# The first projection chunk of a transformer kernel, split in two by k and run between the modulation blocks

## What is computed

```python
mod = silu(c) @ w_ada + b_ada                    # 1024 -> 6144, in 12 blocks of 512 columns
shift1, scale1, gate1, shift2, scale2, gate2 = split(mod, 6)
h = rms_norm(x, norm1_g) * (1 + scale1) + shift1
proj = h @ w_in                                  # 1024 -> 5120, in 10 chunks of 512 columns
q_sb, k_sb, v_sb, q_mb, k_mb, v_mb, g_sb, g_mb = split(proj, ...)
...                                              # two attentions, gates, w_out, 64-expert mixture
...                                              # second block: mixer, memory attention, 16-expert mixture
```

## Time and profile before

| | |
|---|---|
| median of 3 runs | 1556.61 us (1556.6 to 1557.11) |
| the profiled execution, its own time | 1556.61 us |
| its span | 1554.8 us |
| PE busy | 1323.6 us (85%) |
| DVE busy | 545.9 us (35%) |
| ACT busy | 407.1 us (26%) |
| mean granted clock of TensorE | 0.929 |
| DMA | 337 GB/s on the mean over the span |

### The profile page before, as it was taken

One profiled execution on the slowest core, in us unless ns is written; L12 is line 12 of the kernel. 1 busy time (PEld: TensorE's weight loads), 2 busy tenths in 40 slices (PEclk: granted clock), 3 DMA queues, 4 the chain that ended last, 5 costly groups with the idle time before them and its releaser, 6 DMA issues.

```text
span 1554.8 us, 24390 instructions
## 1 busy us (share of the span) xinstructions
PE 1323.6 (85%) x10184; PEld 900.3 (58%) x10184; DVE 545.9 (35%) x1197; ACT 407.1 (26%) x624; POOL 0.2 (0%) x4
## 2 busy tenths in 40 slices
PE   6999998999999999999699999999666657557556
PEld 2888896656666665555488999999323113113112
DVE  3546665343333232321474775753301001001001
ACT  3457743111111111111264346453201000000001
POOL 0000000000000000000000000000000000000000
PEclk8999999899999999999999999999889678788878
DMA  9884759699999999999933544447999999999996
GB/s 364 275 290 172 279 198 403 274 393 385 422 421 415 420 416 420 416 418 421 389 139 114 212 163 163 164 165 292 409 422 417 422 421 418 422 422 419 422 422 250
DMA packets 119321, 523.53 MB, mean 337 GB/s; under 512 B 11032, under 2 KB 15544, under 8 KB 72120
## 3 DMA queue, kind: packets, MB, share of 16 engines
q1 hardware_dynamic: 115952, 519.17, 84.0%
q10 hardware_dynamic: 3272, 2.96, 0.6%
HBM read 520.85 MB, written 1.24 MB: 336 GB/s over the span
## 4 chain that ended last, share of the span: by engine, by line
PE 61%; DMA 17%; SPq 15%; DVE 3%; ACT 2%; issue 2%; DVEq 0%; ACTq 0%
PE psum L1975 17%; PE psum L2425 10%; SPq L663 7%; PE psum L2493 5%; SPq L670 5%; DMA ring<-in_w_up_e_dram 4%; DMA arena<-in_w_exp_down_dram 4%; PE psum L2361 4%; DMA ring<-in_w_exp_up_dram 4%; PE psum L2350 2%; DMA ring<-in_w_exp_down_dram 2%; SPq L674 2%; PE psum L2885 2%; PE psum L2222 1%; PE psum L1983 1%
## 5 line engine op out<-in xcount | busy, mean ns | idle before, releaser
L1975 PE MATMUL psum<-arena_r,ring_r 128*128 128x256 f32 x2400 | 289.0, 281 | 6.0 <-DVE arena_r L1145 3.1
L1975 PEld LDWEIGHTS psum<-arena_r,ring_r 128*128 128x128 f32 x2400 | 283.1, 188 | 12.2 <-issue 7.5
L2425 PE MATMUL psum<-ring,arena 128*32 128x256 f32 (+1 forms) x2304 | 183.9, 390 | 11.2 <-DMA ring<-in_w_up_e_dram 10.4
L1138 DVE TENSOR_TENSOR ring_r<-ring,ring_r 128x1024 fp32r<-128x1024 f32 x140 | 163.2, 1221 | 69.6 <-ACT ring_r L759 68.8
L2425 PEld LDWEIGHTS psum<-ring,arena 128*32 128x32 f32 (+1 forms) x2304 | 111.0, 123 | 76.2 <-issue 20.2
L2885 PE MATMUL psum<-ring,arena 128*32 128x512 f32 x720 | 109.5, 738 | 51.6 <-DMA ring<-in_w_exp_up_dram 46.3
L759 ACT ACTIVATE ring_r<-ring 128x1024 fp32r<-128x1024 f32 x140 | 137.5, 1050 | 27.8 <-DMA ring<-in_w_in_dram 13.4
L2902 PE MATMUL psum<-ring,arena 128*32 128x512 f32 x384 | 76.8, 834 | 66.1 <-DMA ring<-in_w_exp_down_dram 47.6
L2493 PE MATMUL psum<-ring,arena 128*32 128x512 f32 (+1 forms) x544 | 91.0, 617 | 3.4 <-DMA ring<-in_w_down_e_dram 2.5
L2885 PEld LDWEIGHTS psum<-ring,arena 128*32 128x32 f32 x720 | 22.2, 123 | 114.7 <-DMA ring<-in_w_exp_up_dram 64.5
L2902 PEld LDWEIGHTS psum<-ring,arena 128*32 128x32 f32 x384 | 18.7, 142 | 119.3 <-issue 89.8
(11 more groups left out here) (410 smaller groups left out, 1457.0 us busy)
## 6 DMA issues: line engine op xcount, KB each, us to landing
ring<-in_w_gate_e_dram SPq DMA_DIRECT2D x64, 1024.0 KB, 15.1
ring<-in_w_up_e_dram SPq DMA_DIRECT2D x64, 1024.0 KB, 14.3
ring<-in_w_down_e_dram SPq DMA_DIRECT2D x60, 1024.0 KB, 14.4
ring<-in_w_exp_gate_dram SPq DMA_DIRECT2D x45, 1024.0 KB, 26.2
ring<-in_w_exp_up_dram SPq DMA_DIRECT2D x45, 1024.0 KB, 26.0
ring<-in_w_exp_down_dram SPq DMA_DIRECT2D x40, 1024.0 KB, 26.6
ring<-in_w_in_dram SPq DMA_DIRECT2D x19, 2048.0 KB, 8.9
ring<-in_w_ada_dram SPq DMA_DIRECT2D x12, 2048.0 KB, 13.5
```

The lines of the kernel that those rows point to most:

```text
L1138: V.tensor_tensor(lo, whole, hi.bitcast(F32), ALU.subtract).then_inc(w_low, 1)
L1975: ins = product(lambda a_, b_, k, first, last: mm(ps[:, t * T:(t + 1) * T], a_[:, k, c], b_[:, k, :], start=first, stop=last), w, x, None ...
L2425: ins = mm(psum[c, 5, 256 * g:256 * g + 256], xg1[:, k, P * j + width * b:P * j + width * (b + 1)], weight(g, e, k), start=(k == 0), stop= ...
```

## The change

The four modulation blocks and the first projection chunk are loaded and multiplied in another order.

- SP issues ada0, ada1, the first half of in0 (k-tiles 0 to 3), ada2, ada3, the second half of in0. The blocks ada2 and ada3 go to two places in the arena that are free then (`ada_away`: buffers 11 and 12, and 4 and 5), not to the ring. So the ring's list is two slots shorter from there on, and in1 lands in slots that were never used. The load of the memory tokens, which go to buffer 11, waits for ada2's product.
- PE does ada0 and ada1 with their columns, then four matmuls 128x256 whose result is thrown away (`idle_products`), then the k-tiles 0 to 3 of in0 in three portions (24, 12 and 12 matmuls) with ada2 and ada3 between them, then k-tiles 4 to 7 (48).
- ACT copies ada2 and ada3 out behind the high parts of the first half, not ahead of them.

The core of the diff:

```diff
-CHUNKS_A = [("w_ada", 512 * ADA_ORDER[_j], 512, 8) for _j in range(ADA_FIRST)]
+ADA_RING = 2
+CHUNKS_A = [("w_ada", 512 * ADA_ORDER[_j], 512, 8) for _j in range(ADA_RING)]
...
+        ada_away = [buf(11, SLOT), buf(4, SLOT)]
...
+            for n in range(ADA_RING):
+                load(ring[:, SLOT_A[n], :], CHUNKS_A[n], load_a[SLOT_A[n]])
+            first_input_half(0, first_in)
+            for n in range(2):
+                load(ada_away[n], ("w_ada", 512 * ADA_ORDER[ADA_RING + n], 512, 8), load_away[n])
+            first_input_half(1, load_a[SLOT_A[IN_A[0]]])
             for n, spec in enumerate(CHUNKS_A):
+                if n <= IN_A[0]:
+                    continue
...
                 if n == IN_A[3]:
+                    full(sp, "ada2")
                     sp.dma_start(memN, a["mem_columns"].rearrange("p (k t) -> p k t", t=T)).then_inc(mem_in, 16)
...
             rms_act(1, rstd_of(1))
-            for n in range(3):
+            for n in range(2):
                 ada_copy(n)
             act.wait_ge(normed, 1)
             x_high_part("h1", 0)
-            ada_copy(3)
             high(0, (0, 1))
+            for n in (2, 3):
+                ada_copy(n)
             act.wait_ge(normed, 2)
...
+            def idle_products(ps, n):
+
+                for _ in range(n):
+                    mm(ps[:, 0:T], ones, cst[:, 0:T], start=True, stop=True)
...
-            for n in range(ADA_FIRST):
-                if n:
-                    if n == 3:
-                        pe.wait_ge(mod_ready, 1)
-                    columns(n - 1).then_inc(mod_full, 1)
...
+            for n in range(ADA_RING):
                 modulation(n, n)
-            columns(ADA_FIRST - 1).then_inc(mod_full, 1)
...
+                columns(n).then_inc(mod_full, 1)
+            idle_products(start("in0_0"), 4)
+            first_products(0, 0)
+            modulation(2, None)
+            first_products(0, 1, range(1))
+            pe.wait_ge(mod_ready, 1)
+            columns(2).then_inc(mod_full, 1)
+            modulation(3, None)
+            columns(3).then_inc(mod_full, 1)
+            first_products(0, 1, range(1, 2))
+            for j in range(2):
+                first_products(1, j)
```

More of the change, by code:

```diff
@@ L184 @@
 JOBS = ["rel"]
-JOBS += ["ms1", "sum1"] + [f"ada{_j}" for _j in range(ADA_FIRST)]
+JOBS += ["ms1", "sum1", "ada0", "ada1", "in0_0", "ada2", "in0_1", "ada3"]
 for _c in range(6):
-    JOBS += [f"in{_c}_{_j}" for _j in range(2)] + {3: ["ms0"], 4: ["sum0"]}.get(_c, []) + [f"ada{_j}" for _j in ADA_BEHIND.get(_c, ())]
+    JOBS += [f"in{_c}_{_j}" for _j in range(2) if _c] + {3: ["ms0"], 4: ["sum0"]}.get(_c, []) + [f"ada{_j}" for _j in ADA_BEHIND.get(_c, ())]
 for _p in range(PAIRS):
@@ L412, in build @@
         first_in = sem("first_input_half_loaded")
+        load_away = [sem(f"modulation_block_loaded{i}") for i in range(2)]
         load_ahead = sem("block_ahead_loaded")
@@ L537, in load @@
                     sp.dma_start(dst, a["w_gate_sh"][0].rearrange("(k p) f -> p k f", p=P)).then_inc(done, 16)
[L538 to L542, removed]
                 else:
@@ L558, in _, with first_input_half @@
             sp.dma_start(xT, a["x_columns"].rearrange("p (k t) -> p k t", t=T)).then_inc(x_in, 16)
+            def first_input_half(h, landed):
+                dst = ring[:, SLOT_A[IN_A[0]], :].rearrange("p (k c) -> p k c", k=KT)
+                sp.dma_start(dst[:, 4 * h:4 * h + 4, :], a["w_in"][0, 512 * h:512 * h + 512, 0:512].rearrange("(k p) c -> p k c", p=P))\
+                  .then_inc(landed, 16)
+            for n in range(ADA_RING):
[4 more added lines that the diff above has]
+            first_input_half(1, load_a[SLOT_A[IN_A[0]]])
             for n, spec in enumerate(CHUNKS_A):
+                if n <= IN_A[0]:
+                    continue
                 if SLOT_A[n] >= RING:
@@ L2059, in modulation @@
             def modulation(n, place, gives=None):
-                w = chunk_a(place, 512)
+                if ADA_RING <= n < ADA_FIRST:
+                    pe.wait_ge(load_away[n - ADA_RING], 16)
+                    w = ada_away[n - ADA_RING].rearrange("p (k c) -> p k c", k=KT)
+                else:
+                    w = chunk_a(place, 512)
                 if n == 0:
@@ L2075, in modulation @@
                     columns(n - 1, gives=(used_a, 1)).then_inc(mod_full, 1)
-                elif n != ADA - 2:
+                elif n != ADA - 2 and not ADA_RING <= n < ADA_FIRST:
                     full(pe, f"ada{n}")
@@ L2093, in _ @@
             norm_total(1, part_x)
-            for n in range(ADA_FIRST):
-                if n:
-                    if n == 3:
-                        pe.wait_ge(mod_ready, 1)
-                    columns(n - 1).then_inc(mod_full, 1)
-                modulation(n, n)
-            columns(ADA_FIRST - 1).then_inc(mod_full, 1)
[L2102 to L2121, removed]
@@ new lines, in _, with first_products @@
+            n0 = IN_A[9] - 8
+            def first_products(half, j, ts=range(2)):
+                hi, lo = PARTS["h1"]
+                w = chunk("a", IN_A[0], whole=False)
+                name = f"in0_{j}"
+                ps = bank(name) if half or j == 0 or ts[0] else start(name)
+                for t in ts:
+                    cols = slice((2 * j + t) * P, (2 * j + t + 1) * P)
+                    for k in range(4 * half, 4 * half + 4):
+                        if j == 0 and t == 0 and k % 2 == 0:
+                            pe.wait_ge(x_low, 4 * PART_AT["h1"] + k // 2 + 1)
+                            pe.wait_ge(w_low, k // 2 + 1)
+                        for i, (a_, b_) in enumerate(((w[0], hi), (w[0], lo), (w[1], hi))):
+                            ins = mm(ps[:, t * T:(t + 1) * T], a_[:, k, cols], b_[:, k, :], start=(t == 0 and k == 0 and i == 0),
+                                     stop=(k == KT - 1 and i == 2), skip_group_check=True)
+                if half:
+                    done(ins, name)
@@ L2125, in _ @@
                 w = chunk("a", IN_A[c], whole=False)
-                if c == 0:
-                    project_by_halves(w)
                 for j in range(2):
```

## The result

The change is slower, by 0.2 to 0.3%. In the first set of runs its median was 1562.81 us (1559.34 to 1563.65, 6 runs) against 1556.64 us before (1556.44 to 1557.11, 6 runs), a ratio of 1.0033, 95% interval 1.0021 to 1.0045. So the first set puts the change at +6.2 us and the second at +3.0, and the forecast of +4.0 (1560.6) lies between them; the first median alone lies 0.4 us above the range. They come from one trace of each kernel, though, and traces of one kernel differ too.

The account below looks back on a forecast made before the run. The prediction took the modulation weights' loads, then PE from 35.77 us on, to bound the kernel. in0's end moves from 49.63 to 53.6, +4.0 us, all passed on: 1556.61 + 4.0 = 1560.6 us, range 1556.8 to 1562.4.

Parts of the forecast that it names:

- one sign of being wrong that the prediction names: Behind in0: the prediction is wrong if later stages don't keep the shift; no size of its own.
- The path: In in0: the second half of h waits for ada3's later columns, PE idles 3.8 us, in0 ends 4.0 us later.
- the forecast of 53.6 us for in0's end: End of in0: last 48 products from 45.5 us, 24 slow and 24 fast, end at 53.6 against 49.63 before.
- The chain of DVE, ACT and DVE, 5.2 us: Ahead of each half of in0: from the columns' end to PE's first product takes 5.2 us.
- The first 24 products start at 28.1: Start of in0: DVE's step at 22.8 plus 5.3 gives 28.1 us, 7.7 us ahead of 35.77.
- 2.7 slow and 12 fast: 4.1 us: First 24 products of in0: 12 at the slow clock in 2.7 us, 12 fast in 1.4, ending at 32.2.
- The last 48 products, 8.1 us: Second half of in0: slow clock after PE's idling, 24 products slow in 5.3 us and 24 fast in 2.8.
- The price: ada3 is now behind them on PE. This is the term that decides.: PE before in0's second half: ada3's columns end at 40.3, 5.0 us later, 2.7 by the load alone.
- I pass on all of it: Behind in0's end: later stages, expert loads included, start later by the whole shift, so +4.0 us reaches the end.
- my rival: From about 311 us: expert loads set the end, their start isn't moved, shift vanishes: 1556.6, up to 1558; chance 0.09.
- The edits put at nothing: in1's split, the shorter ring and the memory tokens' wait: each nothing; in1's split, if late, under 1 us.

Follow-up runs that it names:

- e8: The change with the clock raised early, 10 idle products ahead of its first 24 products and 7 ahead of the last 48: 1556.55 us, ratio 1.0001.
- e11: The kernel before with the clock raised early as in e7, but three idle products instead of one just ahead of in0: 1554.96 us, ratio 0.9990.
- e5: The change once more, unaltered, in a second set of runs beside the kernel before: 1560.17 us median of 12, ratio 1.0021.
- e12: e1 (the change's loads, old order of PE and ACT) with idle products in PE's gaps: 1554.95 us, ratio 0.9993.
- e1: The change's loads and places only, with PE and ACT in the old order and no idle products: 1559.7 us, ratio 1.0018.
- e10: e11 with 23 idle products instead of three ahead of in0, a pure delay: 1560.54 us median of 7, 5.6 us above e11.
- e9: The kernel before once more, unaltered, one run with its trace: 1557.29 us.
- e4: The kernel before with idle products between the modulation blocks, 3 behind each of the first three blocks' columns: 1555.55 us, ratio 0.9992.
- e7: The kernel before with the clock raised early by idle products from 10 us on, in the waits for copies and behind columns: 1553.81 us, ratio 0.9980.
- e2: The change without its four idle products: 1560.93 us, ratio 1.0028.
- e3: The change with 11 idle products instead of 4 ahead of the first 24 products, and 8 more ahead of the last 48: 1560.52 us, ratio 1.0017.
- e6: The change with the 12 products between ada2's and ada3's products moved behind ada3's columns: 1560.45 us median of 12.

## Why the prediction was right, and where its sizes were off

The forecast of a small loss is right, and so is the path that leads to it at 50 us. But one sign of being wrong that the prediction names did come true: later stages don't keep the shift. That the time still came out near +4.0 is in part luck, since the error ahead of 50 us and the one behind it have opposite signs.

**The path.** Right. That half of in0 waits for the second half of h, behind ada3's columns, is what the trace of the change shows: columns late, then a wait of 3.84 us for DVE (3.8 predicted), then the last 48. In numbers, at in0's end the change is 6.5 us late (+4.0 predicted). Of this 50.92 - 47.64 = 3.3 us are the order (e8 against e11), and the rest, 3.2 us, the clock: it costs the change 55.94 - 50.92 = 5.0 us and the kernel before 49.47 - 47.64 = 1.8.

Against the forecast of 53.6 us for in0's end the chain of the change has 56.11: 2.8 us from ada3's columns (43.14 where I had 40.3), 0.2 from the chain behind them, less 0.5 for the last 48 products.

**The chain of DVE, ACT and DVE, 5.2 us.** Right: 5.3, from 43.18 to 48.49 in the change, and e8's first products at 28.02 where I had 28.1.

**"The first 24 products start at 28.1".** Mis-sized: 29.47, and 30.71 in e5. I took DVE's start at 22.82 from before as fixed, but it stands behind ada1's products, and these took 3.28 and 3.64 us at the slow clock where the profile of before had 1.92. A duration from one trace was only as good as its clock.

**"2.7 slow and 12 fast: 4.1 us".** Mis-sized: 5.46 us, the end that I had kept as a bound. Both together make 2.7 of the 2.8 us by which ada3's columns ended later (43.14) than predicted (40.3).

**The last 48 products, 8.1 us.** 7.6 us, with a slow part, as predicted, but a shorter one: 3.4 us (49.2 to 52.6) where I had taken 5.3, about 15 products by an estimate at 0.222 us each where I had 24. PE idled 3.84 us there and ran slow behind it. The Trainium skill tells of this in "TensorE: Matmul & The Clock Gate", section "HAM oscillation — how this bites in real kernels": a group of matmuls behind a long wait, there for a load, starts at the half clock. Here the trace agrees in part: the granted clock was 0.50 at 50 to 51 us, but the first 0.7 us of the 48 still ran at 1.00.

**"The price: ada3 is now behind them on PE. This is the term that decides."** At ada3's columns it is right: at the fast clock they end 5.5 us later than in e11, 2.5 by the loads and 3.0 by PE's order, and I had 5.0 and 2.7 of it for the load. At in0's end it has the weights wrong: the loads make 2.4 of the 3.3 us and PE's order 0.9, since DVE did not use early columns at once in the old order (e12). At the slow clock, as in e1, the two can't be told apart.

**"I pass on all of it".** This step failed. The lag of 6.5 us at in0 was 3.8 at 299 us and 2.7 at the span's end, and e10's pure delay of 7.3 was 4.3 at 298 us, 4.7 at the span's end and 5.6 in the medians. In the medians of the change 6.2 us arrived in the first set and 3.0 in the second. What the traces show isn't what my rival named (loads that start regardless). It is the clock in later stages, first of all at the start of the expert stage, where the kernel before, e9 and e11 took 1.7 us more for one group of products. Why the slow stretches fall there is open. It isn't the lateness at in0's end alone, as these two show, whose in0 ends at 53.94 (e1) and at 50.92 (e8):

```profile
294.05 5.35 PE psum L2518 x16
```

```profile
289.22 3.65 PE psum L2528 x16
```

Over all 14 traces the first down products took 5.35 us in the kernel before, e1, e4, e7, e9, e11 and e12, and 3.65 in the change, e2, e3, e5, e6, e8 and e10. No run held the clock there.

**The edits put at nothing** were nothing as far as the traces show: no wait on in1's split stands ahead of in1's first product, and in1 and in2 take 11.2 us each as before (56.11 to 67.30 and on to 78.50 in the chain).

**Was it a useful idea with another help?** With the clock raised early it comes back to the kernel before (e8), but the same help on the kernel before is 2.7 us better still (e7, by medians of 12 runs each). Beside e7 only e11 lies below the kernel before with its whole interval, and that by 1.1 us.

## What to carry to other kernels

When a matmul stream is cut to start earlier, ask what its last piece waits for: work on the first half is worth nothing if the piece that frees the second half moves back by as much, in the queue of loads or on the engine. Look also at what the next engine does when that piece is ready: 3.0 us on the columns came to 0.9 at in0's end here, because DVE was not waiting for them in the old order. Count each new gap of TensorE at the clock behind it, not at the clock of the trace before. Filler products help only if they begin while nothing waits for them; begun at the slow clock just ahead of useful work they cost double and delay it (e3, e4), begun at 10 us they gave 3.4 us (e7), but 1.1 in a second version (e11), so what they are worth is known to a few us only. And a lag read at one place of one trace is not yet a difference in time: e12's 2.4 us at in0's end against e11 did not show in the medians.

## What the runs showed of the hardware

The granted clock of a window stands at 1.00 from the span's start until the first change that the trace records, even where durations say 1.2 GHz: e5's ada1 products took 3.64 us against 1.92. Durations of a known group are the better witness there.

The same kernel spreads by up to 7 us over runs (before: 1553.13 to 1560.14 us in 31 runs), where three runs had agreed within 0.5 and six within 0.7. Traces of one kernel show the clock changing at other moments relative to the work: in the change's two traces the first 24 products took 5.46 us, all slow, and 0.95 and 3.83, the first six of them fast (e5). So a median of a few runs can be off by as much as the effect; the second set of the same change lay 2.6 us below the first.
